# An encoder trunk on one core: scan turns in two banks, low products last, GpSimd with every fourth low weight part in the mixing stage

## The reference

```python
h = rms_norm(x, mix_norm_g[i])
proj = h @ w_in[i]
da_q, da_k, da_v, s_z, s_xbc, s_dt, xa_q, gates = split_cols(proj, IN_SIZES)
y_da = diff_attention(...)                    # 8 heads, two softmax maps each
y_ssm = mamba2_bidir(s_z, s_xbc, s_dt, ...)   # conv, forward and backward scan, gated norm
y_xa = mem_cross_attention(xa_q, rms_norm(mem, ...), w_mem_kv[i])   # 4 heads
merged = g0 * (y_da @ wb_da.T) + g1 * (y_ssm @ wb_ssm.T) + g2 * (y_xa @ wb_xa.T)
x = x + merged @ w_out[i]
h = rms_norm(x, ffn_norm_g[i])
gate, up = split_cols(h @ w_ffn_in[i], (FFN_HIDDEN, FFN_HIDDEN))
x = x + (jax.nn.silu(gate) * up) @ w_ffn_out[i]
```

## Time and profile before

| | |
|---|---|
| median of 3 runs | 1452.82 us (1452.64 to 1454.72) |
| the profiled execution | 1453.53 us |
| its span in the profile | 1451.8 us, mean granted clock 0.994 |
| PE busy | 1423.8 us (98%) |
| DVE busy | 925.5 us (64%) |
| ACT busy | 876.5 us (60%) |
| POOL busy | 356.5 us (25%) |
| moved from and to memory | 255.5 MB, 176 GB/s |

### The profile page before, as it was taken

How to read it: one execution, slowest core, us unless ns; L and a number is a source line. 1 busy time by engine, 2 the same in 40 slices (tenths; PEclk the granted TensorE clock), 3 DMA queues, 4 the chain that set the end, 5 groups by cost and what they waited for, 6 DMA issues and landing times.

```text
span 1451.8 us, 25292 instructions
## 1 busy us (share of the span) xinstructions
PE 1423.8 (98%) x8877; PEld 1269.6 (87%) x8877; DVE 925.5 (64%) x1214; ACT 876.5 (60%) x1408; POOL 356.5 (25%) x170
## 2 busy tenths in 40 slices
PE   7999999999999999999999999999999999999997
PEld 6899888888887889998899998988888788899986
DVE  6468475788995446554434764668889845565553
ACT  6576667886755445445456665678767464544453
POOL 3410000011023444544443000001010234354443
PEclk9999999999999999999999999999999999999999
DMA  7555445465665555557555554463666545555664
GB/s 249 179 176 165 130 118 153 137 219 193 204 187 159 187 171 178 173 175 234 181 184 177 163 160 120 141 175 124 213 209 217 170 151 187 171 175 173 191 229 145
DMA packets 158497, 255.48 MB, mean 176 GB/s; under 512 B 12730, under 2 KB 58924, under 8 KB 158380
## 3 DMA queue, kind: packets, MB, share of 16 engines
q1 hardware_dynamic: 157819, 252.84, 56.1%
q10 hardware_dynamic: 560, 1.18, 0.2%
HBM read 252.80 MB, written 1.18 MB: 175 GB/s over the span
## 4 chain that ended last, share of the span: by engine, by line
PE 96%; issue 1%; DVE 1%; ACT 1%; DVEq 0%; POOL 0%; ACTq 0%; POOLq 0%
PE PS L609 83%; PE S L609 9%; PE S L616 1%; DVE wL L1301 1%; PE S L809 0%; PE S L874 0%; PE S L780 0%; PE S L750 0%; PE S L800 0%; ACT regB L985 0%; DVE scr L1362 0%; POOL wL L1229 0%; DVEq L1377 0%; ACT hH L992 0%; ACT wH L910 0%
## 5 line engine op out<-in xcount | busy, mean ns | idle before, releaser
L910 ACT CAST wH<-w_raw 128x1024 fp32r<-128x1024 f32 x443 | 457.8, 1041 | 437.6 <-PE PS L609 390.9
L1301 DVE TENSOR_TENSOR wL<-w_raw,wH 128x1024 fp32r<-128x1024 f32 (+1 forms) x322 | 445.5, 1388 | 372.9 <-ACT wH L910 356.9
L609 PE MATMUL PS<-hH,wH 128*128 128x256 f32 (+1 forms) x1488 | 426.6, 287 | 0.0
L609 PE MATMUL PS<-hH,wL 128*128 128x256 f32 (+1 forms) x1488 | 420.9, 283 | 0.0
L609 PE MATMUL PS<-hL,wH 128*128 128x256 f32 (+1 forms) x1488 | 420.9, 283 | 0.0
L1229 POOL TENSOR_TENSOR wL<-w_raw,wH 128x1024 fp32r<-128x1024 f32 (+1 forms) x121 | 306.2, 2532 | 407.6 <-ACT wH L910 407.5
L609 PEld LDWEIGHTS PS<-hH,wH 128*128 128x128 f32 (+1 forms) x1488 | 284.2, 191 | 3.2 <-issue 2.6
L609 PEld LDWEIGHTS PS<-hL,wH 128*128 128x128 f32 (+1 forms) x1488 | 284.4, 191 | 0.6
L609 PEld LDWEIGHTS PS<-hH,wL 128*128 128x128 f32 (+1 forms) x1488 | 284.2, 191 | 0.0
L609 PE MATMUL PS<-wH,actH 128*128 128x512 f32 x560 | 223.9, 400 | 0.0
L609 PE MATMUL PS<-wL,actH 128*128 128x512 f32 x560 | 218.5, 390 | 0.0
(11 more groups left out here) (237 smaller groups left out, 1576.6 us busy)
## 6 DMA issues: line engine op xcount, KB each, us to landing
w_raw<-in_w_in_dram SPq DMA_DIRECT2D x192, 512.0 KB
w_raw<-in_w_ffn_in_dram SPq DMA_DIRECT2D x176, 256.0 KB
w_raw<-in_w_branch_dram SPq DMA_DIRECT2D x64, 512.0 KB
w_raw<-in_w_ffn_out_dram SPq DMA_DIRECT2D x44, 512.0 KB
w_raw<-in_w_mem_kv_dram SPq DMA_DIRECT2D x35, 512.0 KB
regA<-cs_rows SPq DMA_DIRECT2D x64, 256.0 KB, 4.8
w_raw<-in_w_out_dram SPq DMA_DIRECT2D x16, 512.0 KB
regA<-in_mem_dram SPq DMA_DIRECT2D x6, 512.0 KB, 4.8
```

What stands on the lines that cost most here:

```text
L609: return nc.tensor.matmul(o, l, r, start=first, stop=last, skip_group_check=True)
L910: nc.scalar.copy(wH[:, slot].rearrange("p k c -> p (k c)")[:, q], raw[:, slot].rearrange("p k c -> p (k c)")[:, q]).then_inc(h_done[slot], 1)
L1301: v.tensor_tensor(wL[:, slot].rearrange("p k c -> p (k c)")[:, q], raw[:, slot].rearrange("p k c -> p (k c)")[:, q], wH[:, slot].rearrange ...
```

## The change

- `SSM_BANK`: the eight turns use banks 0,1,0,1,0,1,2,3 instead of 0,0,0,0,0,1,2,3. `SIDE_USES` follows.
- `unit`: the first products of a unit wait for `h_done` alone; the products with `wL` come last, behind a wait of their own for `l_done`.
- `pool_splits`: the first eight units of a layer are all split by DVE (four of them were POOL's), and in the mixing stage POOL takes every fourth unit (27, 31, ... 123, 25 a layer), which were DVE's.

```diff
-SSM_BANK = (0, 0, 0, 0, 0, 1, 2, 3)
+SSM_BANK = (0, 1, 0, 1, 0, 1, 2, 3)
...
-    return u % 2 == 1 and not mixing
+    return u % 2 == 1 and u >= 2 * RING and (not mixing or u % 4 == 3)
...
-SIDE_USES = [31, 23, 29, 22]
+SIDE_USES = [29, 25, 29, 22]
...
-                pe.wait_ge(l_done[slot], use(lay, u) + extra_u + 2)
+                pe.wait_ge(h_done[slot], use(lay, u) + extra_u + 1)
                 aH_, aL_, a0 = operand(kind)
...
                             mm(o, w_h, aH_[:, k, :], new and m % 2 == 0, False)
                             mm(o, w_h, aL_[:, k, :], False, False)
-                            ins = mm(o, w_l, aH_[:, k, :], False, last_unit and kk == UT - 1)
+                    pe.wait_ge(l_done[slot], use(lay, u) + extra_u + 2)
+                    for m in range(4):
+                        for kk in range(UT):
+                            w_l = wL[:, slot, kk, P * m:P * (m + 1)]
+                            ins = mm(dst[:, T * m:T * (m + 1)], w_l, aH_[:, a0 + UT * c + kk, :], False,
+                                     last_unit and kk == UT - 1)
...
                             mm(o, a_h, wH[:, slot, kk, :], new, False)
                             mm(o, a_l, wH[:, slot, kk, :], False, False)
-                            ins = mm(o, a_h, wL[:, slot, kk, :], False, last_unit and kk == UT - 1)
+                    pe.wait_ge(l_done[slot], use(lay, u) + extra_u + 2)
+                    for t in range(NT):
+                        for kk in range(UT):
+                            a_h = aH_[:, a0 + UT * c + kk, P * t:P * (t + 1)]
+                            ins = mm(dst[:, UC * t:UC * (t + 1)], a_h, wL[:, slot, kk, :], False,
+                                     last_unit and kk == UT - 1)
```

More of the change, by code:

```diff
@@ L683, in unit @@
                             k = a0 + UT * c + kk
-                            w_h, w_l = wH[:, slot, kk, P * m:P * (m + 1)], wL[:, slot, kk, P * m:P * (m + 1)]
+                            w_h = wH[:, slot, kk, P * m:P * (m + 1)]
                             o = dst[:, T * m:T * (m + 1)]
```

## The result

The changed kernel takes 1456.74 us (median of 20 runs, 1454.27 to 1458.89) against 1452.40 (20 runs) before: ratio 1.0028, 95% interval 1.0021 to 1.0035. It is slower by 4.3 us, the side that was forecast and inside the range, but about half of the 8 us forecast.

A forecast was written before the change was run, and what follows sets the result against it. PE, busy 98% of the span, was taken as the bound, with its waits and lost clock. Gains of 13.9 us against costs of 21.9 gave net +8.0: 1461.4 profiled, 1460.7 us for the median, range 1443 to 1469.

The forecast's parts named there:

- What bounds the kernel: Whole kernel: PE is busy 98% of the span; time is its own work plus its waits and the half clock behind them.
- Part 1: Turns of the scan, two banks: the 7.2 us of waits and 5.1 us of clock go, gain 12.3 us.
- Part 2: Units, low products last: the wait before unit 3 goes, gain 1.6 us; 440 waits inside units cost 0.
- Part 3: Mixing stage, 25 more POOL low parts a layer: POOL's work holds DVE, so PE stalls; costs together 21.9 us.
- diag 10: Scan product needing DVE's decay 10: PE stalls 5.4 us once a layer, 10.8 us in all.
- clock behind it: After the stalls at diag 10: the clock drops as before, costing 3.4 and 1.7 us, 5.1 in all.
- 11.3 − 1.7 − 2.4 − 0.4 = 6.8: Ahead of decay 10: POOL's holds, less earlier holds, two splits DVE drops, and gaps or PSUM reads, delay DVE 6.8 us.
- `da_turn` 7: Seventh da_turn, needing DVE's combine: POOL's split of unit 79 and a skip cost 2.1 us a layer, 4.2 in all.
- `cs_turn`: cs_turn, needing three short DVE instructions: near tie with POOL's split of unit 31, 1.7 us or nothing; 0.9 a layer.
- B: Rival, between: diag 10 stalls about 3 us, time about 1450 to 1453; chance 0.15.
- C: Rival, slower still: DVE keeps losing after decay 10, a second stall a layer, 11 us more, 1468 to 1475; chance 0.13.
- D: Rival: the change doesn't do what it says; low parts late in one place only, mid-unit waits may cost 5 us; no chance given.

The follow-up runs named there:

- the run with the wait first: Changed kernel without POOL in the mixing stage, waiting for the low part at the unit's start again, low products still last: 1441.04 us, ratio 0.9916.
- 107 alone: Changed kernel with POOL splitting only unit 107 of the mixing stage: 1440.54 us, ratio 0.9911 to the kernel before.
- the two-bank run: Kernel before with only the turns' banks changed to 0,1,0,1,0,1,2,3 (and SIDE_USES): 1442.42 us, ratio 0.9925.
- the run with all but 103: Changed kernel with the low part of unit 103 alone given back from POOL to DVE: 1451.76 us, ratio 0.9998 to the kernel before.

## Why the prediction was off, point by point

**What bounds the kernel** was right: PE's waits and the clock behind them make the whole difference between the two profiles. Span less waits less clock is 1451.8 − 18.7 − 5.1 = 1428.0 before and 1453.1 − 21.5 − 3.4 = 1428.2 after.

**Part 1** was right in its mechanism, and turn 3 indeed never waits. Its size was 12.3 us and measured 10.1 alone, 11.2 in the changed kernel. Alone, the missing 2.2 us are the longer wait before unit 3 and the clock behind it, which part 2 removes in the changed kernel. Parts 1 and 2 together were forecast at 13.9 us; the spans of the two profiles differ by 13.7 (1451.8 and 1438.1, without POOL in the mixing stage), the medians by 12.6. So the gain was right for the profiled execution, and the term that was too large for the median is most likely its clock, 5.1 us, read from one execution 1.1 us slower than the median of the 20.

**Part 2** had the right sum (1.6; 2.0 measured) by a reason that was half wrong. "With DVE making that low part in 1.2 us too, it is gone surely": DVE alone leaves 1.6 us (the run with the wait first). The late wait is what removes it. Waits inside units at 0 were right, and the 5 us kept for them was not needed. "Worth nothing elsewhere" was right too: with POOL's new units on the kernel before, where PE still asks for the low part at the unit's start, the only wait for one is again that before unit 3, 1.7 us.

**Part 3** was forecast at 21.9 us and costs 16.9. Cost that was 5.0 us too high and gain that was 1.3 too high partly cancel: 4.3 us measured against 8.0. Term by term, from the profile of the changed kernel:

| term | forecast | measured |
|---|---|---|
| diag 10, two layers | 10.8 | 6.1 |
| clock behind it | 5.1 | 3.4 profiled; the median run is 1.9 us slower, cause not shown |
| `da_turn` 7 | 4.2 | 2.7 |
| `cs_turn` | 1.8 | 0 |
| exponential at 253 us | none | 2.0 |

The step that failed is "11.3 − 1.7 − 2.4 − 0.4 = 6.8". The rule under it held: DVE's instructions beside a POOL one are longer by about the overlap (0.69 became 2.69 beside 2.44). What failed is that it was applied to a DVE "without gaps". DVE's row has low parts in it that wait for ACT's casts, and taking one low part out opens a gap in front of the next. Unit 99's split therefore held DVE for 0.2 us instead of 2.4, and its removal brought DVE nothing instead of 1.2. The others held it for less than their length: added up from the lengthened instructions it is 0.8 + 2.0 + 0.6 + 2.9 + 0.6, rounded 7.1, against 8.5 forecast (11.3 less the 2.4 of unit 99 and the 0.4). That a part of each fell between two DVE instructions is likely from the timeline, but wasn't measured by itself. With the 0.2 of unit 99 the line reads 7.3 − 1.7 − 1.2 = 4.4 in place of 6.8. That is what the timeline has: decay 10 is 5.0 us later than before, and 0.6 of it PE itself is late, by the waits upstream. 4.4 − 1.42 = 3.0, and 3.1 was measured, against 5.4 forecast. The second step that failed is a term put at nothing: the exponential at 253 us, 2.0 us in all, for which the prediction has no line; every place that it priced is one at which PE waits for DVE itself.

**`da_turn` 7.** Forecast 2.1 each (its own 3.4 less 1.4 is 2.0), measured 1.3: the split held a DVE instruction of 0.22 us for 1.9 more (2.11, at 284.69) and the skip the combine for 0.7 more (1.58 instead of 0.88), 2.6 in place of 3.4. **`cs_turn`** was called a near tie. It fell to DVE's side: in the changed kernel DVE's three instructions start at 94.02 and POOL's split of unit 31 at 94.25, and the two that are left by then read PSUM (bank `S`) and take 0.28 and 0.29 us as before. The forecast's 0.9 was the mean of two outcomes, so the 0 is the one it called as likely as the other.

**Rivals.** B's 3-us stall at diag 10 is what came, though its time (1450 to 1453) was too low: it left out the wait at the exponential, and its gain of 5.1 us of clock was more than the median run gives back (its own terms add up to +0.2, which is 1453.0 for the median, the upper end). C's second stall at diag 11 doesn't come in the changed kernel; it does come, 0.6 to 1.1 us, in layers in which diag 10 waits 1.1 us or less (0 and 0.3 with 107 alone). That fits a PE which is late by its stall and its low clock, as C's condition says. D is out: the waits inside units cost nothing that can be told.

## What to carry to other kernels

Work that is moved to an engine which blocks another one costs nothing in idle stretches, and up to its whole length where the other is the feeder of a bound engine; of 25 places here, three brought 9 of the 17 us lost. The size of such a stall can't be had by adding the blocker's times: find how far ahead of its deadline the blocked engine is, which of its instructions is next when the blocker starts, how many stand between it and the one that is waited for, and whether the blocked engine is waiting for a third engine anyway. Look at every layer: here the same splits caught different instructions in the two layers. A change of three parts is to be measured in parts: two of these were worth 12.6 us, and the third hid them.

## What the runs showed of the hardware

- The wait that is followed by half clock is shorter than the 3.6 us read before. 2.1 us sufficed in the two-bank run at 24.5 us and in the run with POOL at 99 and 107 in the second layer (clock 0.79 in the window below and 0.87 in the next), 2.2 in the second layer of the run with all but 103. Behind waits of 1.7 us and less no profile here shows a drop.

```profile
1095.00:1100.00 5.00, 3.97 (x17) 3.39 (x18) 4.19 (x6) 3.01 (x4) 0.31 (x1) 0.79 0.18 59
```

- Within a kernel the slower runs mostly have the lower mean clock. Kernels with no wait over 1 us behind the first load scatter by 0.2 to 0.5 us (1439.40 to 1439.87, 1441.96 to 1442.32); those with waits of 3 to 4 us often scatter by 4 to 7 (1449.19 to 1453.25, 1454.27 to 1458.89, and the kernel before 1450.67 to 1457.49). Not always: the changed kernel with one bank has four such waits and scatters by 0.7 us over four runs, the one with POOL's units alone by 1.8 over five. Why these don't is open.
- A small DVE instruction with one input is held by POOL as a large one with two is: the one on line 1486, 128x4, took 1.95 us instead of 0.17 beside POOL's split of 2.40, and the four scalings 4.62 instead of 1.67. One that reads PSUM, at 94.52 us (line 1560), took 0.29 beside a split, as without it.
- POOL's instructions get longer beside DVE's too: a weigh or skip that takes 1.04 us undisturbed took 2.04 at 359.27.
- A satisfied wait inside a run of products costs PE about 1 ns by the one subtraction above, which can't be told from nothing.
